# A gate ahead of the pooling sums, a new order in the first block, and a last column in two token halves

## The reference

```python
def first_block(x, mem, ...):
    h = rms_norm(x, norm_mix)
    aq, ak, av, bq, bk, bv, cq = split(h @ w_in)
    lam = exp(sum(q1 * k1)) - exp(sum(q2 * k2)) + lambda_init
    out_a = rms_norm(diff_attention(rms_norm(aq), rms_norm(ak), av, lam)) * (1 - lambda_init)  # 4 heads
    out_b = dilated windows, 3 groups x 4 heads, merged by softmax of their log-sum-exp
    out_c = attention of cq to 256 memory tokens (ck, cv = rms_norm(mem) @ w_mem_kv)          # 4 heads
    gates = sigmoid(h @ w_gate + b_gate)                       # 3 x 1024 columns
    x = x + sum(gates * (out_a, out_b, out_c) @ w_branch) @ w_out
    return x + (silu(h2 @ w_ffn_gate) * (h2 @ w_ffn_up)) @ w_ffn_down

def second_block(x, mem, ...):
    for l in range(2):
        x = x + 0.5 * swiglu(rmsnorm(x))                       # hidden width 2816
        q, f, i, g, u = split(rmsnorm(x) @ w_in[l])            # 5 x 512 columns
        o_a = rmsnorm(hgrn2(q, f, i)) * norm_g * silu(g)       # 4 heads, linear recurrence
        o_b = (trailing mean of u over 2/4/8/16 tokens - u) @ pool_w * pool_scale
        x = x + concat(o_a, o_b) @ w_out[l]
        x = x + cross_attention(rmsnorm(x), rmsnorm(mem))      # 4 heads of width 256
        x = x + 0.5 * swiglu(rmsnorm(x))
    return rmsnorm(x, final_norm)
```

## Time and profile before

| what | value |
|---|---|
| median of 3 runs | 3341.74 us (3341.23 to 3343.29) |
| the profiled execution's own time | 3344.93 us |
| its span | 3343.0 us |
| mean granted clock of TensorE | 0.992 |
| PE busy | 3254.0 us, 97% |
| DVE busy | 1719.4 us, 51% |
| ACT busy | 1120.0 us, 34% |
| DMA | 313.33 MB, mean 94 GB/s |
| raw weights, 512 KB | 553 transfers, median 3.3 us to land |
| x again, 2048 KB | 1 transfer, 9.4 us to land |

### The profile page before, as it was taken

The page is one execution under the profiler, slowest core; times in us unless marked ns, Lnnn a source line. Parts: engine busy times, 40 slices in busy tenths (PEclk is TensorE's granted clock), DMA queues, the critical chain, the costliest instruction groups (busy, mean ns, idle before and its releaser), DMA issues.

```text
span 3343.0 us, 39817 instructions
## 1 busy us (share of the span) xinstructions
PE 3254.0 (97%) x14944; PEld 2665.3 (80%) x14944; DVE 1719.4 (51%) x2483; ACT 1120.0 (34%) x1771; POOL 0.2 (0%) x4
## 2 busy tenths in 40 slices
PE   9999999999999999999899999999999989999998
PEld 7777777778888888887787888888888878778887
DVE  6664445555444554346664554344543666554542
ACT  4654544532222322232343322232223233332221
POOL 0000000000000000000000000000000000000000
PEclk9999999999999999999999999999999999999999
DMA  4323323232222222232231222222223223122222
GB/s 141 101 78 101 97 73 113 64 115 98 94 95 101 95 94 100 95 110 70 89 101 57 95 94 99 96 95 98 97 95 112 80 66 117 57 89 95 99 95 88
DMA packets 88536, 313.33 MB, mean 94 GB/s; under 512 B 9952, under 2 KB 10336, under 8 KB 87904
## 3 DMA queue, kind: packets, MB, share of 16 engines
q1 hardware_dynamic: 82224, 294.69, 26.4%
q10 hardware_dynamic: 6192, 16.97, 1.6%
HBM read 309.52 MB, written 2.10 MB: 93 GB/s over the span
## 4 chain that ended last, share of the span: by engine, by line
PE 92%; DVE 3%; ACT 2%; issue 1%; DMA 1%; SPq 0%; DVEq 0%; ACTq 0%
PE ps L985 28%; PE ps L987 28%; PE ps L986 28%; PE ps L1256 1%; PE ps L1160 1%; PE ps L1171 1%; ACT stage_sq L1396 1%; PE ps L1286 1%; PE ps L1060 0%; PE ps L1149 0%; DMA x_res<-in_x 0%; PE ps L1267 0%; PE ps L1203 0%; PE ps L1207 0%; ACT whi L1302 0%
## 5 line engine op out<-in xcount | busy, mean ns | idle before, releaser
L985 PE MATMUL ps<-x_hi,whi 128*128 128x512 f32 x2400 | 946.4, 394 | 0.0
L987 PE MATMUL ps<-x_hi,wlo 128*128 128x512 f32 x2400 | 935.2, 390 | 0.0
L986 PE MATMUL ps<-x_lo,whi 128*128 128x512 f32 x2400 | 934.5, 389 | 0.0
L1302 ACT ACTIVATE whi<-raw 128x1024 fp32r<-128x1024 f32 (+1 forms) x555 | 583.5, 1054 | 997.4 <-DMA raw<-in_weights 993.2
L1540 DVE TENSOR_TENSOR wlo<-raw,whi 128x1024 fp32r<-128x1024 f32 x553 | 675.0, 1223 | 424.3 <-ACT whi L1302 415.6
L985 PEld LDWEIGHTS ps<-x_hi,whi 128*128 128x128 f32 x2400 | 451.4, 188 | 97.2 <-issue 5.4
L986 PEld LDWEIGHTS ps<-x_lo,whi 128*128 128x128 f32 x2400 | 451.4, 188 | 94.9 <-issue 2.4
L987 PEld LDWEIGHTS ps<-x_hi,wlo 128*128 128x128 f32 x2400 | 450.8, 188 | 94.9
L985 PE MATMUL ps<-h_hi,whi 128*128 128x512 f32 x880 | 342.3, 389 | 0.0
L986 PE MATMUL ps<-h_lo,whi 128*128 128x512 f32 x880 | 342.3, 389 | 0.0
L987 PE MATMUL ps<-h_hi,wlo 128*128 128x512 f32 x880 | 342.3, 389 | 0.0
(11 more groups left out here) (278 smaller groups left out, 3350.3 us busy)
## 6 DMA issues: line engine op xcount, KB each, us to landing
raw<-in_weights SPq DMA_DIRECT2D x553, 512.0 KB, 3.3
bias<-in_biasB ACTq DMA_DIRECT2D x16, 384.0 KB, 3.2
bias<-in_biasA ACTq DMA_DIRECT2D x16, 256.0 KB, 3.1
mem_raw<-in_mem ACTq DMA_DIRECT2D x3, 1024.0 KB, 7.2
x_res<-in_x SPq DMA_DIRECT2D x8, 256.0 KB, 6.6
x_res<-in_x ACTq DMA_DIRECT2D x1, 2048.0 KB, 9.4
out_x<-x_res SPq DMA_DIRECT2D x8, 256.0 KB, 2.0
raw<-in_weights SPq DMA_DIRECT2D x2, 256.0 KB, 4.3
```

Source lines behind the costliest of these rows:

```text
L985: pe.matmul(out, hi, xhi, start=start, stop=False)
L986: pe.matmul(out, hi, xlo, start=False, stop=False)
L987: return pe.matmul(out, lo, xhi, start=False, stop=stop)
L1302: return act.activation(out, in_, ACT.Copy, scale=scale)
```

## The change

The change has nine parts.

1. **Opening.** The small matmul for `lam` becomes a step of its own after all key columns; `consts` comes after the second of them.
2. **First attention's output.** ACT copies the bank to SBUF, which frees it; `oa_hi` and `oa_lo` are made from that copy.
3. **Dilated attention.** `S1` is free when its own two blocks are copied (`(i, "far")`), not when all six are.
4. **Head 3 and after.** Five gates, the fetch of the memory and four of its norm steps move between head 3's tiles; three more gate buffers (`GX`) make room; the two merges stand back to back; gate 5 goes between keys and values of the third attention.
5. **Third attention.** Odd tiles are turned in `T1`.
6. **`w_out`.** x comes back chunk by chunk, each as soon as its `y_lo` is made, and columns 0 and 1 begin with their first seven steps.
7. **HGRN `between`.** The column of the pooling comes first, then the turn and gate of the first head, then the sums, then `hprep(1)`.
8. **Cross attention.** A third query column stands ahead; the rest move to (3,7,11,15,20), then (28,30,32).
9. **End.** The last column runs as two halves of 256 tokens, 66 matmuls each; the final norm and the output transfers run by halves, the first half's between the products of the second.

```diff
     a_keys[0]()
-    step("consts")
     step("setup")
...
     a_keys[1]()
+    step("consts")
...
     a_keys[3]()
+    step("lam")
...
+                if m > 1:
+                    step("reload", m=m - 2)
...
+    b_work = [b_parts[12:20], b_parts[20:28], b_parts[28:37],
+              b_parts[37:38] + [memload] + b_parts[38:] + [gate_b_mem(m) for m in range(5)]]
...
+    for jj in range(2):
+        pair_b(jj)
+        for go in memparts[4 + 2 * jj:6 + 2 * jj]:
+            go()
     memsum()
-    gate_b(5)
...
-    for go in c_keys + c_values:
+    for go in c_keys + [lambda: gate_b(5)] + c_values:
...
+        products(0, 0, NF)
+        square(0)
+        sq = s.steps[-1][1]["sq"]
+        products(1, 0, 6)
+        form = sums(0)
+        products(1, 6, 13)
+        step("hturn", id=("F", n, 0), form=form, slot="O")
+        products(1, 13, NF)
+        step("final", n=n, half=0, slot="O")
+        square(1)
+        form = sums(1)
+        step("hturn", id=("F", n, 1), form=form, slot="T0")
+        step("final", n=n, half=1, slot="T0")
...
             first[1]()
+            pool_column(3)
+            first[2]()
+            step("poolsum", l=l, g=3)
             hprep(1, evacuated)
-            pool_job(3)
-            first[2]()
...
-        for go in queries[:2]:
+        for go in queries[:3]:
...
-               queries[2:] + [start for start, _ in begun], places=(2, 5, 9, 13, 17, 21, 28, 30, 32))
+               queries[3:] + [start for start, _ in begun], places=(3, 7, 11, 15, 20, 28, 30, 32))
...
+        def turn_slot(a):
+            return "T1" if a["kind"] == "C" and a["i"] % 2 else "T0"
...
                     if a["kind"] == "B":
-                        free["S1"] = ("pt", i)
+                        free["S1"] = ("pt", (i, "far"))
...
                     if role["dst"][0] == "OA":
-                        copy(OAH[:, role["dst"][1], :], src, gain_of(role["gain"])).then_inc(*sig("ohi", role["id"]))
+                        whole = AOS[role["dst"][1] % 2].rearrange("p t c d -> p (t c d)")
+                        copy(whole, src, gain_of(role["gain"])).then_inc(*sig("hq", role["id"]))
+                        act.wait_ge(*on("hq", role["id"]))
+                        copy(OAH[:, role["dst"][1], :], whole).then_inc(*sig("ohi", role["id"]))
...
-                    act.wait_ge(*on("ylo", DC - 1))
-                    act.wait_ge(*own("act"))
-                    act.dma_start(X[:, :, :], dram["x"]).then_inc(sems["d_reload"], 16)
+                    m = a["m"]
+                    act.wait_ge(*on("ylo", m))
+                    act.dma_start(X[:, m, :], dram["x"][:, m, :]).then_inc(d_x[m], 16)
```

More of the change, by code:

```diff
@@ L91, in step @@
     def step(self, kind, /, **a):
-        if kind in ("refresh", "memfresh", "hsq"):
+        if kind == "refresh" and a.get("half"):
+            a["sq"], a["sq_free"] = (self.nsq - 1) % SQS, None
+        elif kind in ("refresh", "memfresh", "hsq"):
             a["sq"] = self.nsq % SQS
@@ L469, in build_schedule, with merged @@
     step("ylo", m=DC - 1)
-    step("reload")
+    step("reload", m=DC - 2)
+    step("reload", m=DC - 1)
     norm = 1
+    def merged(m):
+        return dict(rhs="y", n=T, evac="resid", m=m, c=1.0, need={k: [("ylo", k)] for k in range(DC)} if m == 0 else {})
+    begun = [s.column_parts("w_out", 0, m, tuple(range(DC)), DC - 1, **merged(m)) for m in range(2)]
+    for start, _ in begun:
+        start()
     for m in range(DC):
-        need = {k: [("ylo", k)] for k in range(DC)} if m == 0 else {}
-        j = column("w_out", 0, m, rhs="y", n=T, evac="resid", m=m, c=1.0, need=need)
+        j = begun[m][1]() if m < 2 else column("w_out", 0, m, **merged(m))
         step("refresh", n=norm, m=m, gain="norm_ffn", need=("evac", j))
@@ L489, in ffn, with closing, products, square @@
             s.unit(w2, l, order[u:u + UT])
-        for m in range(DC):
+        last = gain_next == "final_norm_2"
+        for m in range(DC - last):
             j = s.job(t1 + m * NF, NF, rhs="h", n=T, evac="back" if back else "resid", m=m, c=c, first=(m == 0), norm=n)
             step("refresh", n=n + 1, m=m, gain=gain_next, need=("x", m) if back else ("evac", j))
+        if last:
+            closing(t1 + (DC - 1) * NF, c, n + 1, gain_next)
+    def closing(tile0, c, n, gain):
+        a = dict(tile0=tile0, nk=NF, rhs="h", n=T // 2, evac="resid", m=DC - 1, c=c)
+        jobs = (s.njobs, s.njobs + 1)
+        s.njobs += 2
+        s.open_units((tile0 + NF - 1) // UT + AHEAD)
+        s.settle()
+        def products(half, k0, k1):
+            step("job", j=jobs[half], k0=k0, k1=k1, held=not half, at=half * (T // 2), **a)
+        def square(half):
+            step("evac", j=jobs[half], held=not half, at=half * (T // 2), **a)
+            step("refresh", n=n, m=DC - 1, half=half, gain=gain, need=("evac", jobs[half]))
+        def sums(half):
+            form = s.hsums(("F", n, half), "ones", T // 2, D, s.steps[-1][1]["sq"] if half else sq)
+            s.settle()
+            return form
+        products(0, 0, NF)
[11 more added lines that the diff above has]
+        step("final", n=n, half=1, slot="T0")
     ffn("w_ffn_gate", "w_ffn_up", "w_ffn_down", 0, 1.0, 1, "ffn1_norm_2_0", back=True)
@@ L898, in job_done @@
             end = a["tile0"] + a["nk"]
-            return on("unit_free", end // UT - 1) if end % UT == 0 else on("job_mid", a["j"])
+            return on("unit_free", end // UT - 1) if end % UT == 0 and not a.get("held") else on("job_mid", a["j"])
         def stage(a):
@@ L967, in _ @@
                 sp.dma_start(raw[u % RING][:, :], dram["weights"][u]).then_inc(raw_landed[u % RING], 16)
-            for m in range(DC):
-                sp.wait_ge(*on("fin", m))
-                sp.dma_start(dram["out"][:, m, :], X[:, m, :]).then_inc(sems["d_out"], 16)
-            sp.wait_ge(sems["d_out"], 16 * DC)
+            for half in range(2):
+                tokens = slice(half * (T // 2), (half + 1) * (T // 2))
+                for m in range(DC):
+                    sp.wait_ge(*on("fin", (m, half)))
+                    sp.dma_start(dram["out"][:, m, tokens], X[:, m, tokens]).then_inc(sems["d_out"], 16)
+            sp.wait_ge(sems["d_out"], 2 * 16 * DC)
         @block.tensor
@@ L1090, in _ @@
                         else:
-                            xhi, xlo = (x[:, kk, 0:n] for x in parts[a["rhs"]])
+                            xhi, xlo = (x[:, kk, a.get("at", 0):a.get("at", 0) + n] for x in parts[a["rhs"]])
                         mm = three(out, hi, lo, xhi, xlo, k == 0, k == a["nk"] - 1)
-                        if c == UT - 1:
+                        if c == UT - 1 and not a.get("held"):
                             mm.then_inc(*sig("unit_free", tile // UT))
```

108 lines of the change are left out of this document (60 added, 48 removed).

## The result

The changed kernel takes 3307.56 us (median of 4 runs, 3306.48 to 3309.93); the kernel before, on the same chips, 3342.51 (4 runs). The ratio is 0.9896 with a 95% interval of 0.9879 to 0.9913: 35 us less, where 47 were forecast. The forecast was 3294.6 with a range of 3286 to 3309, so the time lies in the range, 1.4 us from its upper end. The profiled execution took 3309.93 us with a span of 3307.8.

What follows compares the result with a forecast made beforehand. PE, busy 97% of the span, was taken as the bound, so only its waits and half-clock products could go. Terms summed to 47.1 us off the 3341.7 median, giving 3294.6 us, range 3286 to 3309.

Steps and rivals of the forecast that it cites:

- between: HGRN mixer, twice: PE's wait for the gate falls from 9.2 to 1.1 us, half clock behind it shrinks; -17.4 in all.
- Head 3 and after: Dilated attention's end: moved gates cover PE's waits, 14.1 us with restarts and slow clock, less new waits; -11.5 us.
- New: ... 1.4; three smaller ones 1.2: At head 3: new waits, 1.4 us for the last turn behind its score, 1.2 for three smaller ones.
- Cross attention: Both layers: one more query column ahead removes the 6.3 us of waits for x_q and some turn waits; -6.8 us.
- two fifths of the turns' waits gone: Cross attention: 1.3 of the 3.2 us that turns wait outside the third attention go.
- Output's turn: First attention's output: DVE's step of 0.8 us leaves the path, ACT's extra copies cost up to 0.5; -0.5 us.
- S1: Dilated attention: freeing the buffer after its own two blocks removes two of three waits, 2.9 us in all; -1.1 us.
- The opening: Start: the 3.5 us wait for lam goes, 5.5 us gained with clock, 2.1 given back; -3.4 us.
- (a): Rival: DVE gives gains back at the mixer (4.3 us per layer), head 3 and query columns; 3312 us, 13 in 100.
- (b): Rival: weight loads pace the last column's half-width products, 9.6 us more; 3304 us, 4 in 100.
- (c): Rival: another input of the mixer's output matmuls is late too, so its part gives nothing; 3312 us, 3 in 100.
- (d): Rival: the denser stream is granted less clock over all of PE's time; slower, 3357 us at 0.973, 1 in 100.

Runs made afterwards that it cites:

- d_old: Changed kernel with head 3 of the dilated attention and the fill behind it as before the change; one profile, 4.3 us more at third attention's first score.
- norm_late: Changed kernel with the four norm products of group c_q on DVE put one product of steps later; 3303.08 us against 3307.56.
- banks: Changed kernel with other bank numbers for third attention's values and, in the first layer, cross attention's first values; 3304.20 us against 3308.23.
- best: Changed kernel with norm_late, banks and the first attention's output turned as before the change; 3300.37 us, ratio 0.9868 to the kernel before.
- x_old: Changed kernel with the cross attention as before the change, two query columns ahead; one profiled execution, 1.7 us more per layer.
- x_early: Changed kernel with two query columns ahead of the cross attention and the other six at earlier places; 3312.58 us against 3308.23.

## Why the prediction was right, and where it was off

- **As a whole** the time lies in the range, but near its end, and nearly all large errors point one way: removed waits were counted rightly, new ones too low. What went better than forecast (x by chunks, the second mixer, the half clock in the third attention) made part of it good, and that was not foreseen.
- **The mechanism and the largest term were right.** `between` was forecast at 8.7 per layer and measured at 7.5 and 9.2. What failed there is the place of the give-back: I had 0.5 at the pool matmul (0.3 came) and 1.1 at the levels (0.5 came in the second layer). In the first 1.7 came at the evacuation of `x_k`, 28 us behind the gate, further than I had followed DVE's row.
- **Head 3 and after was mis-sized**, -11.5 for -4.8, the largest error. With the half clock in the third attention, which this term did not count, it is -6.9. The removed waits were right: `d_old` has the same 9 us. The step that failed is "New: ... 1.4; three smaller ones 1.2". I followed PE's row and laid the gates over its waits, but not DVE's row between them. The norm of `c_q` ahead of the last score (3.6 us with its half clock, shown by `norm_late`) and the bank clash (1.8, shown by `banks`) make most of the 6.7 missing; in `best`, with both mended, it is 5.6. Where the last 1.1 went was not found.
- **Cross attention was mis-sized**, -6.8 for -3.3. The waits for `x_q` went as forecast, 3.1 per layer. The step that failed is what I set beside them: two fifths of the turns' waits gone, 0.8 per layer new, and 0.8 of restarts. `x_old` and `x_early` show that the same columns cover ACT's copies: PE's waits for ACT rose from 1.2 to 2.7 us per layer, 1.5 more, and so 1.7 were left.
- **Output's turn and `S1`** had the wrong sign or were next to nothing, some 1.2 off each. In both I counted what a bank's release gives and not who waits for ACT or DVE next.
- **The opening** was right where the clock stood: with the wait of 1.3 for the squares and 0.5 for the root (forecast 2.1 together) it leads by 2.2 at 91 us in the profile after, and in `norm_late`, whose opening is the same, by 3.8. Most of the difference is the stretch at clock 0.56 at 28 to 31 us.
- **x by chunks** gave 3.8 for 2.0: the wait went as forecast (2.15), and with it 1.6 us of half clock behind it, which I had left out there though I counted it elsewhere.
- **`T1` and the halves** came out as forecast.
- Of the rivals, (a) happened in a milder form: at head 3, in the cross attention, and at the mixer of the first layer, there 1.7 us at `x_k`. Its 4.3 per layer right behind the gate did not come. (b), (c) and (d) did not happen. The mean granted clock is 0.996 and rose.

## What to carry to other kernels

Work laid over another engine's wait has its own rows on that engine; read the row of the engine that is waited for up to the next thing it must deliver, as carefully as the one that waits. Where banks are dealt out by a running number, a clash can sleep: here neither number changed, and one column moved right ahead of a group, or an evacuation later against PE, was enough. Look at the banks of neighbours whenever the order or the pace of either side changes. A wait's price is its length, the restart and, at times, the stretch at half clock behind it, and the last is not constant even for the same instructions.

## What the runs showed of the hardware that I had not expected

The same wait of 1.77 us, in kernels with the same instructions up to there, is followed by 6 us at mean clock 0.72 in some executions and at 1.00 in others. In `x_old` the clock fell behind a wait of 0.57 us only, with 16 small products between:

```profile
2607.32 0.58 PE L1086 MATMUL ps<-ones,sq_sum 128*128 128x1 f32 x4 [0.57 <-ACT rstd_mem L1492]
```

```profile
2609.00:2613.00 4.00, 4.00 (x16) 3.23 (x16) 3.91 (x7) 2.10 (x3) 0.00 (x0) 0.59 0.05 19
```

It cost 1.6 us. The changed kernel has the same wait at 2607.29 us and no such stretch. Differences of one to two us between two profiles are therefore read from the seams that have no such stretch between them, not from the spans.
